# Expert stage of an encoder block: two products with the same weights made one of 480 columns

## What is computed

```python
idx = jnp.take_along_axis(cidx.reshape(TB, PH, K * K), pos, axis=-1)
g = jax.nn.softmax(top_s, axis=-1).astype(xb.dtype)
u = expert_u[idx]
a = jax.nn.gelu(jnp.einsum('td,thkd->thk', xb, u), approximate=False)
return jnp.einsum('thk,thkd->td', g * a, expert_v[idx])
```

## Time and profile before

| | |
|---|---|
| median of 3 runs | 969.53 us (969.27 to 971.58) |
| span of the profiled execution | 971.0 us |
| expert stage, GELU of tile 0 to GELU of tile 127 | 249.1 to 608.8 us |
| GELU of tile 44 to that of tile 113 | 371.24 to 569.28 us |
| PE busy, share of the span | 99% |
| DVE, ACT, POOL busy | 78%, 57%, 34% |
| DMA packets | 254.60 MB, mean 262 GB/s |

### The profile page before, as it was taken

The page is one execution under the profiler, slowest core; times in us unless marked ns, Lnnn a source line. Parts: engine busy times, 40 slices in busy tenths (PEclk is TensorE's granted clock), DMA queues, the critical chain, the costliest instruction groups (busy, mean ns, idle before and its releaser), DMA issues.

```text
span 971.0 us, 23876 instructions
## 1 busy us (share of the span) xinstructions
PE 961.8 (99%) x8425; PEld 942.9 (97%) x8425; DVE 758.4 (78%) x1604; ACT 556.3 (57%) x996; POOL 325.5 (34%) x199
## 2 busy tenths in 40 slices
PE   9999999999999999999999999999999999999997
PEld 9989899999999999999999999999999999999997
DVE  7988868879799977787777765777777777677775
ACT  6556854666654657676676664555455455454545
POOL 0000000077876868888888870010001000000000
PEclk9999999999999999999999999999999999999999
DMA  8877778756677989999999998999999999899881
GB/s 298 273 222 206 193 206 233 237 175 210 194 227 237 253 244 283 292 279 293 287 262 290 278 277 251 343 328 325 289 321 317 338 290 310 263 310 289 262 257 45
DMA packets 134083, 254.60 MB, mean 262 GB/s; under 512 B 29856, under 2 KB 78880, under 8 KB 133744
## 3 DMA queue, kind: packets, MB, share of 16 engines
q1 hardware_dynamic: 112048, 235.30, 76.8%
q0 software_dynamic: 21376, 17.12, 8.6%
q10 hardware_dynamic: 576, 1.06, 0.3%
HBM read 227.07 MB, written 26.35 MB: 261 GB/s over the span
## 4 chain that ended last, share of the span: by engine, by line
PE 82%; DMA 7%; DVE 5%; issue 3%; ACT 2%; SPq 1%; ACTq 0%; DVEq 0%
PE pO L1427 37%; PE pTT L1726 18%; PE pM L1726 17%; DMA raw<-in_stream 6%; PE pO L1706 4%; DVE wlos L909 2%; PE pSS L1492 1%; DMA a_scratch<-ast 1%; PE pSS L1752 1%; PE pSS L1648 1%; ACT whis L646 1%; ACT ast L792 1%; DMA raw<-in_vrows 1%; DMA xcol<-in_xcol 0%; PE pM L1531 0%
## 5 line engine op out<-in xcount | busy, mean ns | idle before, releaser
L646 ACT ACTIVATE whis<-raw 128x1024 fp32r<-128x1024 f32 x326 | 344.7, 1058 | 246.5 <-PE pM L1726 165.7
L1427 PE MATMUL pO<-xhi,whis 128*128 128x240 f32 (+1 forms) x1040 | 288.4, 277 | 0.1
L1427 PE MATMUL pO<-xlo,whis 128*128 128x240 f32 (+1 forms) x1040 | 286.0, 275 | 0.3 <-issue 0.3
L1427 PE MATMUL pO<-xhi,wlos 128*128 128x240 f32 (+1 forms) x1040 | 285.9, 275 | 0.0
L909 DVE TENSOR_TENSOR wlos<-raw,whis 128x1024 fp32r<-128x1024 f32 x173 | 209.6, 1219 | 29.4 <-ACT whis L646 24.7
L1323 DVE TENSOR_TENSOR wlos<-raw,whis 128x1024 fp32r<-128x1024 f32 x125 | 153.1, 1225 | 85.8 <-ACT whis L646 73.5
L626 POOL DMA_INDIRECT g_scratch<-small x112 | 195.7, 1747 | 42.6 <-issue 32.3
L1427 PEld LDWEIGHTS pO<-xhi,whis 128*128 128x128 f32 x1040 | 196.2, 189 | 2.7 <-issue 2.3
L1427 PEld LDWEIGHTS pO<-xlo,whis 128*128 128x128 f32 x1040 | 196.3, 189 | 0.5 <-issue 0.4
L1427 PEld LDWEIGHTS pO<-xhi,wlos 128*128 128x128 f32 x1040 | 196.3, 189 | 0.2 <-issue 0.2
L587 POOL TENSOR_TENSOR wlos<-raw,whis 128x1024 fp32r<-128x1024 f32 x29 | 70.0, 2421 | 214.4 <-ACT whis L646 214.4
(11 more groups left out here) (290 smaller groups left out, 1825.8 us busy)
## 6 DMA issues: line engine op xcount, KB each, us to landing
raw<-in_stream SPq DMA_DIRECT2D x199, 512.0 KB
raw<-in_vrows SPq DMA_DIRECT2D x128, 512.0 KB
a_scratch<-ast SPq DMA_DIRECT2D x128, 120.0 KB
held<-a_scratch SPq DMA_DIRECT2D x128, 120.0 KB
g_scratch<-ghot SPq DMA_DIRECT2D x32, 256.0 KB, 4.4
held<-x_scratch SPq DMA_DIRECT2D x16, 512.0 KB
held<-g_scratch SPq DMA_DIRECT2D x124, 64.0 KB
biasm<-in_bias SPq DMA_DIRECT2D x8, 256.0 KB, 5.6
```

What stands on the lines that cost most here:

```text
L646: act.activation(whi[s], raw[s][:], ACT.Copy).then_inc(hi_ready, 1)
L1427: last = pe.matmul(dst, st, mv, start=(c == 0 and q == 0), stop=(c == len(terms) - 1 and q == 2))
```

## The change

The change works on the tiles i >= 44 (WIDE = 44) of the expert stage, 84 tiles. `xhi` and `xlo` become two halves of one buffer `xpair`. For each chunk the two products with `whi` become one product with 480 columns, whose moving operand is two runs of 240 columns, 8 KB apart; it writes the left half (high inputs) and the right half (low inputs) of 480 columns of the bank. The product of `wlo` with `xhi` stays and adds to the left half. A tile has 16 products in place of 24, and its result is the sum of the two halves: ScalarE copies the right half to SBUF (`take_half`), VectorE adds the left half out of PSUM (`add_halves`), and ScalarE's GELU reads the sum from SBUF. The GELU of tile i stands in ScalarE's turn i+1, behind `hi_at` of that turn, ahead of `take_half(i+1)`. `add_halves(i)` stands in VectorE's turn i+1, behind `low_w`. TensorE's wait for the bank is now for `halves_added` of tile i-2 in place of its GELU. SP's list is unchanged.

```diff
+WIDE = 44
-            xhi = sbs(uphase, "xhi", [P, C, T], F32R)
-            xlo = sbs(uphase, "xlo", [P, C, T], F32R)
+            xpair = sbs(uphase, "xpair", [P, 2, C, T], F32R)
+            xhi, xlo = xpair[:, 0], xpair[:, 1]
...
-            upad = sbs(uphase, "upad", [P, 2, T])
+            halves = sbs(uphase, "halves", [P, 2, T])
...
             def gelu(i):
-                act.wait_ge(tile_done, T_U + i + 1)
+                if i < WIDE:
+                    act.wait_ge(tile_done, T_U + i + 1)
+                else:
+                    act.wait_ge(halves_added, i - WIDE + 1)
                 if i >= 2:
                     act.wait_ge(a_stored[i % 2], 16 * (i // 2))
-                act.activation(ast[i % 2][:, 0:NU], pO[i % 2][:, 0:NU], ACT.Gelu).then_inc(evac_act, 1)
+                act.activation(ast[i % 2][:, 0:NU], pO[i % 2][:, 0:NU] if i < WIDE else halves[:, i % 2, 0:NU], ACT.Gelu).then_inc(evac_act, 1)
+
+            def take_half(i):
+                act.wait_ge(tile_done, T_U + i + 1)
+                if i - 2 >= WIDE:
+                    act.wait_ge(evac_act, act_takings(T_U) + i - 2 + 1)
+                act.activation(halves[:, i % 2, 0:NU], pO[i % 2][:, NU:2 * NU], ACT.Copy).then_inc(half_taken, 1)
...
-                gelu(i)
+                if i >= WIDE:
+                    if i > WIDE:
+                        gelu(i - 1)
+                    take_half(i)
+                else:
+                    gelu(i)
...
             for i in range(NE_TILES):
                 u_tile(i)
+            gelu(NE_TILES - 1)
             w_hi(1, 1)
...
+            def add_halves(i):
+                dve.wait_ge(half_taken, i - WIDE + 1)
+                dve.tensor_tensor(halves[:, i % 2, 0:NU], pO[i % 2][:, 0:NU], halves[:, i % 2, 0:NU], ALU.add).then_inc(halves_added, 1)
...
                 low_w(T_U + i + LO_LEAD)
+                if i - 1 >= WIDE:
+                    add_halves(i - 1)
...
+            add_halves(NE_TILES - 1)
             low(0, 0)
...
+            def u_product(i, s, c):
+                if i < WIDE:
+                    for q, (st, mv) in enumerate(((whi, xhi), (whi, xlo), (wlo, xhi))):
+                        last = pe.matmul(pO[i % 2][:, 0:NU], st[s][:, c, :], mv[:, c, 0:NU], start=c == 0 and q == 0, stop=c == C - 1 and q == 2)
+                    return last
+                two = pO[i % 2][:, 0:2 * NU].rearrange("p (q n) -> p q n", q=2)
+                pe.matmul(two, whi[s][:, c, :], xpair[:, :, c, 0:NU], start=c == 0, stop=False)
+                return pe.matmul(pO[i % 2][:, 0:NU], wlo[s][:, c, :], xhi[:, c, 0:NU], start=False, stop=c == C - 1)
...
-                tile_wait(T_U + i)
+                if i - 2 >= WIDE:
+                    pe.wait_ge(lo_ready, T_U + i + 1)
+                    pe.wait_ge(halves_added, i - 2 - WIDE + 1)
+                else:
+                    tile_wait(T_U + i)
```

More of the change, by code:

```diff
@@ L425, in build @@
         ysum_ready = sem("ysum_ready")
+        half_taken = sem("half_taken")
+        halves_added = sem("halves_added")
         a_stored = [sem(f"a_stored{s}") for s in range(2)]
@@ L1696, in _ @@
                 s = (T_U + i) % RING
-                tile_wait(T_U + i)
+                if i - 2 >= WIDE:
[3 more added lines that the diff above has]
+                    tile_wait(T_U + i)
                 if k is None:
-                    split_product(pO[i % 2][:, 0:NU], [(whi[s][:, c, :], wlo[s][:, c, :], xhi[:, c, 0:NU], xlo[:, c, 0:NU]) for c in range(C)]).then_inc(tile_done, 1)
+                    for c in range(C):
+                        last = u_product(i, s, c)
+                    last.then_inc(tile_done, 1)
                 else:
@@ L1704, in _ @@
                         for c in range(half * C // 2, (half + 1) * C // 2):
-                            for q, (st, mv) in enumerate(((whi, xhi), (whi, xlo), (wlo, xhi))):
-                                last = pe.matmul(pO[i % 2][:, 0:NU], st[s][:, c, :], mv[:, c, 0:NU], start=c == 0 and q == 0, stop=c == C - 1 and q == 2)
+                            last = u_product(i, s, c)
                         if half:
```

## The result

The kernel after takes 1033.34 us (median of 4 runs, 1031.85 to 1037.65) against 969.77 before: 1.066 times the time, 95% interval 1.065 to 1.068. The forecast had the direction and the mechanism and less than half of the size: 27 us, where 64 came.

The account below looks back on a forecast made before the run. TensorE was taken as the bound. Tiles 44 to 113 +26.3 us, the next 14 tiles 0 and the handover +1.2 made 998.5 on the profiled 971.0; less 1.5 to the median, 997 us, range 968 to 1022.

Parts of the forecast that it names:

- TensorE's bound and its gain: Expert stage: TensorE sets the pace; 672 chunks with 480-column products gain 2 to 16 us, taken as 7.
- The rival by which the split product would lose: TensorE: a 480-column product with two separated runs costs 256 ns or more, 20 us lost, 990 us; chance 0.03.
- The loop of two tiles: SP's queue: load n+2 waits for GELU n-4, behind raw tile n's copy; 3.25 us a tile, 983 to 1022 us, chance 0.62.
- GELU to load: Part of the SP loop: start of a GELU to the load behind its store, 0.76 us plus 0.06 for x rows.
- copy to GELU: Part of the loop on ScalarE: raw tile's copy start to the GELU's, 0.98 us plus 0.22 for small copies.
- D: Raw weight tiles: time from a load's issue to its copy's start, taken as 4.5 us, bounds 4.0 to 5.2.
- the other two terms: In the loop, copy start to GELU and GELU to load, together 2.0 us for two tiles.
- The low end of the range: For the loop: 983 us, from a tile of 3.05 us; the whole forecast range began at 968.
- The tail and the handover: Last 14 tiles: 39.4 us against 39.5, so 0; TensorE idle before the next phase: +1.2 us.
- The in-order wait on VectorE: Late raw tiles stall TensorE through low_w and the add: +15 us, 978 us; chance 0.17.
- The floor of the DMA engines at 970 us: Expert stage: DMA share 0.99 holds the stretch at 198 us, so about 970 us; chance 0.08.
- All four rivals: TensorE's gain without the loop 963 us (0.10), DMA floor 970 (0.08), VectorE order 978 (0.17), costly split product 990 (0.03).

Follow-up runs that it names:

- both_no_rows: After with stores one load later, the add ahead of low_w, no 12 gathers of 512 KB, and x rows cut to 64 columns in the stage; 967.70 us.
- before_lag4: The kernel before with each store issued one load earlier from tile 44 on; 1025.85 us, 1.056.
- gelu_moved: The kernel before with only the GELU moved one turn later, behind hi_at, from tile 44 on; 1026.44 us, 1.058.
- both44: The kernel after with the add ahead of low_w and stores one load later for tiles 44 to 127 alone; 971.49 us, 1.001.
- filled: The kernel after with six products of 240 columns into an unused bank added behind each tile from 46 on; 1032.57 us, 1.063.

## Why the prediction was right or wrong

**TensorE's bound and its gain: right.** I had 335 ns for a chunk going to between 312 and 332, and took 7 us in all. Starts in both_no_rows, TensorE's timeline:

```profile
499.75 0.38 PE L1726 MATMUL pO<-xpair,whis 128*128 128x480 f32 x1
...
500.07 0.38 PE L1726 MATMUL pO<-xpair,whis 128*128 128x480 f32 x1
500.29 0.27 PE L1727 MATMUL pO<-xpair,wlos 128*128 128x240 f32 x1
500.40 0.38 PE L1726 MATMUL pO<-xpair,whis 128*128 128x480 f32 x1
```

A chunk takes 0.325 us here, and 0.067/8 = 8.4 ns less than before by the tiles, 327. The rule of the Trainium skill (TensorE: Matmul & The Clock Gate, "Back-to-back issue gap") gives 305 for the chunk and a saving of 2.5; the trace differs on both. That section gives this rule for a product by itself and says that in a stream the loading of the weights counts too, so the prediction held it to a case that it is not meant for. The rival by which the split product would lose is out.

**The loop of two tiles: right.** GELU to load stayed at 0.88 with the x rows in it (forecast 0.82), copy to GELU 1.28 (1.20), the share of the DMA engines fell (0.9 was forecast, 0.83 came), and before_lag4 and gelu_moved show the loop without the rest.

**The step that failed: the size of D.** I took 4.5 us with bounds of 4.0 and 5.2, and it is 5.08, or 5.0 over the copies that waited. At 69 tiles half of 0.58 is 20 us, most of the 24 by which the stretch is over the forecast (248.7 against 224.3); the other two terms, 2.16 for 2.0, are 5.5. The base was wrong: the earlier trace rows gave 4.0 as the shortest landing, and the prediction called D "near 4.0" in the whole stretch from 280 to 354 us. The trace of before had the better figure there. ScalarE's waits in that stretch, and the load and the copy of another tile in it (tile 27, matched by counting both in order):

```profile
ACT whis L646 <- DMA raw<-in_stream: 4.8, 8, 1.2
...
308.08 0.43 SPq L470 DMA_DIRECT2D raw<-in_stream  x1
...
314.01 1.06 ACT L646 ACTIVATE whis<-raw 128x1024 fp32r<-128x1024 f32 x1 [0.78 <-DMA raw<-in_stream]
```

Tile 27 took 5.9 us, the longest of the eight that waited; their mean is 5.0 and the shortest 4.0. With 5.0 the pair would have been 7.0 us and the tile 3.5. I took a value just over the shortest on the ground that fewer loads would be open, and that relief didn't come. Why it didn't stays open. Of the other traffic I had thought the scatter the lesser and the x rows and gathers the greater part; that order is right (0.09 and 0.33), but together they are 0.4 us.

Three smaller things in the working were off. The low end of the range goes by a tile of 3.05 us, while the bound D = 4.0 gives 3.0. The end of a load 3.2 us after its issue can't be read from the earlier trace rows: the slices behind that moment still stand at 147 to 335 GB/s. And the price that the Trainium skill puts on a DMA (DMA: Bandwidth & Descriptors, "Anatomy of one DMA") is given there for DMAs that GpSimd issues, while SyncE issues these loads. The shortest of the waited loads in after had a D of 3.5 us, where that price gives 3.2.

**The tail and the handover: wrong, and small.** With D = 3.9 I gave the last 14 tiles 39.4 us; they took 42.4, two tiles in 6.1, and D over the copies of tiles 118 to 131, which stand ahead of these GELUs, was 4.5 in the mean, even with the scatter over. The wait before the next stage's first product was 4.1 us, not 1.2:

```profile
665.95 0.38 PE L1768 MATMUL pTT<-vhi,whis 128*128 128x240 f32 x1 [4.07 <-DVE vlo L1338]
```

The low part stood behind VectorE's last add. That waited for ScalarE's last half copy, and this stood behind the copy of a raw tile that landed late. ScalarE's and VectorE's timelines:

```profile
663.54 1.06 ACT L649 ACTIVATE whis<-raw 128x1024 fp32r<-128x1024 f32 x1 [3.31 <-DMA raw<-in_vrows]
...
665.17 0.41 DVE L1356 TENSOR_TENSOR halves<-pO,halves 128x240 f32<-128x240 f32 x1 [3.37 <-ACT halves L805]
```

A load of the next stage was late, then, and `take_half(127)`, the add and `vlo` followed it one after the other. Also not in the sum were 3.2 us up to the GELU of tile 44, of which a part is only that this GELU comes later in its tile.

**The rivals.** The in-order wait on VectorE is real and costs 9 us once the loop is open, against the 15 I gave it as a case of its own; in the kernel after it is hidden. The floor of the DMA engines at 970 us is near where both44 ends (971.5), though that the DMA engines hold it there isn't shown alone. Neither is where the kernel after is. All four rivals were under the forecast, and my range ended at D = 5.2 with nothing above it for the tail, the handover and the start, which together were 7 us over.

## What to carry to other kernels

Before an instruction is moved to a later place, follow what waits for its result through the queues: here a store, and behind it in the same list the load that feeds the ring. Count how many tiles lie between a load and the next load that depends on it; the time from issue to use, divided by that number, is a floor for the tile, and going from three to two cost 55 us with no engine any busier. For the size, take the mean of the landings that were waited for and not the shortest: here that mean was 5.0 us in the trace of before, in the nearest stretch, and 5.0 in that of after.

## What the runs showed of the hardware

In the kernel after the granted clock of TensorE fell to its lower level several times during the stage, each time in or behind a gap in TensorE's work. One of them:

```profile
429.97 0.27 PE L1726 MATMUL pO<-xpair,wlos 128*128 128x240 f32 x1
433.02 0.46 PE L1725 MATMUL pO<-xpair,whis 128*128 128x480 f32 x1 [2.78 <-DVE halves L1356]
433.31 0.28 PE L1726 MATMUL pO<-xpair,wlos 128*128 128x240 f32 x1
433.43 0.38 PE L1725 MATMUL pO<-xpair,whis 128*128 128x480 f32 x1
...
434.35 0.41 PE L1726 MATMUL pO<-xpair,wlos 128*128 128x240 f32 x1
434.55 0.62 PE L1725 MATMUL pO<-xpair,whis 128*128 128x480 f32 x1
...
435.16 0.62 PE L1725 MATMUL pO<-xpair,whis 128*128 128x480 f32 x1
435.58 0.40 PE L1726 MATMUL pO<-xpair,wlos 128*128 128x240 f32 x1
435.78 0.61 PE L1725 MATMUL pO<-xpair,whis 128*128 128x480 f32 x1
```

TensorE was idle for 2.8 us, ran some 1.3 us at the full level (2.4 GHz) and then at 1.2 GHz, where a chunk takes 0.62 us (435.16 to 435.78) in place of 0.33; the first products at that level are those at 434.35 and 434.55. A mean of 0.95 over 248.7 us is some 25 us at the lower level. It cost nothing that can be seen here, as filled shows, because TensorE was waiting anyway. I had not looked for it: the clock was 1.00 in every stretch of before.
